# Keeping the last three items' rows apart, and scaling and storing the sums one item earlier

## What is computed

```
y = x + attention(...)                         # these rows start the sums, acc
h = rms_norm(y); gates = softmax(top-4 of 32 of (h @ router_w + router_b))
for expert e, for the rows that chose e:
    gu  = h_rows @ w_gu[e] + b_gu[e]           # 1024 -> 2048
    act = min(gu_a, 7) * sigmoid(1.702 * min(gu_a, 7)) * (clip(gu_b, -7, 7) + 1)
    acc[rows] += gate * (act @ w_down[e] + b_down[e])
out = acc * rsqrt(mean(acc ** 2) + 1e-5) * final_norm_g
```

## Time and profile before

| | |
|---|---|
| median of 3 runs | 2220.52 us (2220.04 to 2221.96) |
| the profiled execution, its own time | 2224.10 us |
| its span, first to last instruction | 2222.3 us |
| TensorE busy | 2179.7 us, 98% of the span |
| mean granted TensorE clock | 0.992 of full speed |
| VectorE, ScalarE, GpSimd busy | 1384.9, 568.5, 253.1 us |
| DMA | 489.55 MB, mean 220 GB/s |

### The profile page before, as it was taken

The page is one execution under the profiler, slowest core; times in us unless marked ns, Lnnn a source line. Parts: engine busy times, 40 slices in busy tenths (PEclk is TensorE's granted clock), DMA queues, the critical chain, the costliest instruction groups (busy, mean ns, idle before and its releaser), DMA issues.

```text
span 2222.3 us, 39903 instructions
## 1 busy us (share of the span) xinstructions
PE 2179.7 (98%) x14798; PEld 1896.8 (85%) x14799; DVE 1384.9 (62%) x2827; ACT 568.5 (26%) x1247; POOL 253.1 (11%) x229
## 2 busy tenths in 40 slices
PE   9999999999999999999999999989999999999996
PEld 7444554566579999999999999989999999999996
DVE  3352232677667778776877678745766566667566
ACT  2113121345312222222222222211212122222123
POOL 1000000022140010101010101000100000011003
PEclk9999999999999999999999999999999999999998
DMA  8000001211158999898999899956977788789687
GB/s 319 33 38 1 0 11 65 88 43 58 49 206 280 313 313 306 288 304 298 307 300 325 272 305 312 315 192 221 307 246 229 235 283 284 251 288 314 221 301 287
DMA packets 244660, 489.55 MB, mean 220 GB/s; under 512 B 24399, under 2 KB 24607, under 8 KB 244452
## 3 DMA queue, kind: packets, MB, share of 16 engines
q1 hardware_dynamic: 223684, 452.48, 58.9%
q0 software_dynamic: 20704, 36.29, 6.9%
q10 hardware_dynamic: 224, 0.16, 0.0%
HBM read 477.64 MB, written 49.63 MB: 237 GB/s over the span
## 4 chain that ended last, share of the span: by engine, by line
PE 94%; issue 2%; DMA 2%; DVE 1%; ACT 1%; POOL 0%; SPq 0%; POOLq 0%; DVEq 0%
PE PS L1042 68%; PE PS L690 14%; PE PS L898 5%; PE PS L698 1%; PE PS L871 1%; PE PS L838 1%; PE PS L860 1%; PE PS L917 0%; PE PS L705 0%; DVE unit L1599 0%; DMA acc_dram<-pairA,cur_y 0%; DMA pairB<-acc_dram 0%; DMA out_dram<-pairB 0%; DMA unit<-acc_dram,cur_y 0%; PE PS L783 0%
## 5 line engine op out<-in xcount | busy, mean ns | idle before, releaser
L1042 PE MATMUL PS<-pairA,unit 128*128 x12288 | 1543.5, 289 | 16.4 <-issue 15.3
L1042 PEld LDWEIGHTS PS<-pairA,unit 128*128 128x128 f32 x12288 | 1538.3, 191 | 21.7 <-issue 20.6
L1810 DVE STREAM_TRANSPOSE unit<-unit 32x512 f32<-32x512 f32 x496 | 315.3, 636 | 8.2 <-DMA unit<-h_dram,cur_x 1.4
L1829 DVE STREAM_TRANSPOSE pairA<-unit 32x512 f32<-32x512 f32 x496 | 315.3, 636 | 6.9
L1349 ACT ACTIVATE unit<-PS,cur_b 128x256 f32<-128x256 f32 x256 | 107.2, 470 | 398.2 <-PE PS L1042 353.0
L690 PE MATMUL PS<-pairA,unit 128*128 128x512 f32 (+1 forms) x464 | 202.9, 594 | 0.0
L1330 ACT ACTIVATE unit<-unit 128x512 f32<-128x512 f32 x128 | 80.5, 630 | 470.2 <-DVE unit L1868 470.1
L1336 ACT ACTIVATE unit<-PS,cur_b 128x256 f32<-128x256 f32 x256 | 107.2, 470 | 308.7 <-PE PS L1042 304.9
L583 POOL DMA_INDIRECT acc_dram<-pairA,cur_y x62 | 99.3, 1601 | 701.8 <-ACT pairA L1309 691.6
L690 PEld LDWEIGHTS PS<-pairA,unit 128*128 128x128 f32 (+1 forms) x464 | 85.6, 187 | 101.1 <-issue 100.3
L1883 DVE TENSOR_SCALAR unit<-unit 128x512 f32<-128x512 f32 x128 | 54.5, 426 | 158.6 <-ACT unit L1336 155.3
(11 more groups left out here) (259 smaller groups left out, 1194.2 us busy)
## 6 DMA issues: line engine op xcount, KB each, us to landing
unit<-in_expert_w_gu_dram SPq DMA_DIRECT2D x256, 1024.0 KB, 5.4
unit<-in_expert_w_down_dram SPq DMA_DIRECT2D x128, 1024.0 KB, 7.9
unit<-in_w_in_dram SPq DMA_DIRECT2D x6, 2048.0 KB, 14.7
pairB<-in_x_dram SPq DMA_DIRECT2D x16, 512.0 KB, 12.0
unit<-in_w_out_dram SPq DMA_DIRECT2D x2, 2048.0 KB, 8.9
h_dram<-pairA SPq DMA_DIRECT2D x8, 512.0 KB, 2.6
acc_dram<-pairB SPq DMA_DIRECT2D x8, 512.0 KB
pairB<-acc_dram SPq DMA_DIRECT2D x8, 512.0 KB, 8.0
```

The source lines that it names most:

```text
L1042: ins = pe.matmul(ps[:, ITEM * (j % 2):ITEM * (j % 2) + w], slot_w[s][:, k, P * j:P * j + P], xa_cols[:, ITEM * kd:ITEM * kd + KD * ITEM + ...
L1810: ins = dve.transpose(cols[:, :, :, 32 * q:32 * q + 32], rows[:, :, :, 32 * a:32 * a + 32])
L1829: ins = dve.transpose(rows[:, :, :, 32 * a:32 * a + 32], cols[:, :, :, 32 * q:32 * q + 32])
```

## The change

- Three items' rows are kept apart: item 29's too, in `old_rows`, with its indices copied to `old_y`. So the sums are read back one item earlier, with items up to 28 in them: SP loads tiles 0 to 2 among item 29's down slabs and 3 to 7 among item 30's first five slabs.
- ACT squares the tiles in item 30: three after `take_y`, two in its second pass, three behind its last read of the up half. DVE makes the mean and scales tiles 0 to 5 between item 30 and item 31, tile 6 in item 31's first pass and tile 7 in its second. In item 31 ACT squares `old_rows` (in place of six tiles), and DVE scales them after tile 7.
- SP stores the eight tiles among item 31's slab loads: tile 0 behind slab (0, 2), 1 and 2 behind (0, 3), 3, 4, 5 behind (1, 0), (1, 1), (1, 2), 6 behind (2, 0) and 7 behind (2, 2). Each store waits in SP's queue until its tile is scaled, and the next slab's load stands behind it.
- POOL gathers `old_rows` in item 30, after the adds have landed and ahead of its `y_sent`, makes one more power ahead of item 31's adds, and at the end writes three sets of rows in place of two, each after the one before has landed (`y_out`). A memset of `old_rows` is added ahead of POOL's loop.
- Item 30 is written out behind the loop on DVE, ACT and POOL, as item 31 was, and item 29 and 30 on SP. TensorE's program is unchanged.

```diff
@@ -200,6 +200,7 @@
         last_rows, prior_rows = kn(unit[5][:, 0:2048], 2), kn(unit[5][:, 2048:4096], 2)
+        old_rows = kn(unit[1][:, 1024:3072], 2)
@@ -430,7 +431,11 @@
-            def item_weights(i, e, sums=()):
+            def store_tile(t):
+                sp.wait_ge(out_ready, t + 1)
+                sp.dma_start(out_rows[t], acc[:, t, :]).then_inc(out_sent, 16)
+
+            def item_weights(i, e, sums=(), done=()):
@@ -439,33 +444,36 @@
                                 if t == 0:
-                                    sp.wait_ge(y_sent, last)
+                                    sp.wait_ge(y_sent, i + 2)
                                 sp.dma_start(acc[:, t, :], acc_dram[P * t:P * t + P, :]).then_inc(rows_in[t], 16)
+                        for t, place in done:
+                            if place == (p, s):
+                                store_tile(t)
...
                     load_slab(p, s, 0)
-            with sp.Fori(1, N_EXP - 2) as i:
+            with sp.Fori(1, N_EXP - 3) as i:
...
             item = sp.alloc_register("sp_item")
-            sp.reg_mov(item, N_EXP - 2)
+            sp.reg_mov(item, N_EXP - 3)
...
                 with sp.Fori(0, MAX_EXTRA):
-                    i = sp.snap(item, min_val=N_EXP - 2, max_val=ITEMS - 2)
-                    with sp.If(i + 2 < last):
+                    i = sp.snap(item, min_val=N_EXP - 3, max_val=ITEMS - 3)
+                    with sp.If(i + 3 < last):
...
                         sp.reg_add(item, item, 1)
-            prior = sp.snap(item, min_val=N_EXP - 2, max_val=ITEMS - 2)
-            e = sp.value_load(item_e[0:1, bass.ds(prior, 1)], min_val=0, max_val=N_EXP - 1)
-            item_weights(prior, e, ((0, (2, 1)), (1, (2, 2)), (2, (2, 3))))
-            e = sp.value_load(item_e[0:1, bass.ds(prior + 1, 1)], min_val=0, max_val=N_EXP - 1)
-            item_weights(prior + 1, e, ((3, (0, 0)), (4, (0, 1)), (5, (0, 2)), (6, (0, 3)), (7, (1, 0))))
-            for t in range(NT):
-                sp.wait_ge(out_ready, t + 1)
-                sp.dma_start(out_rows[t], acc[:, t, :]).then_inc(out_sent, 16)
+            old = sp.snap(item, min_val=N_EXP - 3, max_val=ITEMS - 3)
+            loads = (((0, (2, 1)), (1, (2, 2)), (2, (2, 3))),
+                     ((3, (0, 0)), (4, (0, 1)), (5, (0, 2)), (6, (0, 3)), (7, (1, 0))), ())
+            stores = ((), (), ((0, (0, 2)), (1, (0, 3)), (2, (0, 3)), (3, (1, 0)), (4, (1, 1)), (5, (1, 2)),
+                               (6, (2, 0)), (7, (2, 2))))
+            for n in range(3):
+                e = sp.value_load(item_e[0:1, bass.ds(old + n, 1)], min_val=0, max_val=N_EXP - 1)
+                item_weights(old + n, e, loads[n], stores[n])
@@ -603,30 +611,46 @@
             last = pool.value_load(n_items[0:1, 0:1], min_val=N_EXP, max_val=ITEMS)
+            pool.memset(old_rows, 0.0)
...
                         i = pool.snap(item, min_val=1, max_val=ITEMS)
-                        with pool.If(i + 1 < last):
+                        with pool.If(i + 2 < last):
...
                             pool.reg_add(item, item, 1)
-            final = pool.snap(item, min_val=N_EXP - 1, max_val=ITEMS - 1)
-            for t in range(NT):
-                pool.wait_ge(rows_in[t], 32)
-            add_to_sums(final)
-            pool.wait_ge(mean_sq, 3 * NT + 1)
-            pool.tensor_tensor(rstd[:, :], ssq[:, :], neg_half[:, :], ALU.pow).then_inc(rstd_ready, 1)
-            pool.wait_ge(y_out, 32 * final)
-            pool.sem_inc(pool_waited, 1)
-            for rows, index, arrived in ((prior_rows, cur_y, prior_in), (last_rows, cur_x, xg_in)):
+
+            def take_rows(rows, index, arrived):
+
+                pool.sem_inc(pool_waited, 1)
...
+
+            prior = pool.snap(item, min_val=N_EXP - 2, max_val=ITEMS - 2)
+            next_rows(prior)
+            for t in range(NT):
+                pool.wait_ge(rows_in[t], 32)
+            add_to_sums(prior)
+            step.do(pool.tensor_copy(old_y[:, :], cur_y[:, :]))
+            pool.wait_ge(y_out, 32 * prior)
+            take_rows(old_rows, old_y, apart_in)
+            pool.sem_inc(y_sent, 1)
+
+            pool.wait_ge(mean_sq, 3 * NT + 1)
+            pool.tensor_tensor(rstd[:, :], ssq[:, :], neg_half[:, :], ALU.pow).then_inc(rstd_ready, 1)
+            pool.wait_ge(apart_in, 32)
+            pool.wait_ge(mean_sq, 3 * NT + 2)
+            pool.tensor_tensor(small[:, 10:12], small[:, 8:10], neg_half[:, 0:2], ALU.pow).then_inc(rstd_ready, 1)
+            add_to_sums(prior + 1)
+            pool.wait_ge(y_out, 32 * prior + 32)
+            take_rows(prior_rows, cur_y, apart_in)
+            take_rows(last_rows, cur_x, xg_in)
@@ -637,21 +661,24 @@
-            pool.wait_ge(mean_sq, 3 * NT + 2)
+            pool.wait_ge(mean_sq, 3 * NT + 3)
...
             for b in range(2):
-                finish_rows(prior_rows, cur_y, b, NT + b + 1)
+                finish_rows(old_rows, old_y, b, NT + b + 1)
+            pool.wait_ge(y_out, 32 * last)
             for b in range(2):
-                pool.wait_ge(mean_sq, 3 * NT + 3 + b)
+                finish_rows(prior_rows, cur_y, b, NT + b + 3)
+            for b in range(2):
+                pool.wait_ge(mean_sq, 3 * NT + 4 + b)
...
                                    ALU.pow).then_inc(rstd_ready, 1)
-            pool.wait_ge(y_out, 32 * last)
+            pool.wait_ge(y_out, 32 * last + 32)
             for b in range(2):
-                finish_rows(last_rows, cur_x, b, NT + 3 + b)
-            pool.wait_ge(prior_in, 32)
+                finish_rows(last_rows, cur_x, b, NT + 5 + b)
+            pool.wait_ge(apart_in, 64)
             pool.wait_ge(xg_in, 32 * last + 64)
-            pool.wait_ge(y_out, 32 * last + 32)
+            pool.wait_ge(y_out, 32 * last + 64)
@@ -1318,17 +1345,21 @@
-            def gate_up(i, first=False, final=False):
+            def gate_up(i, first=False, prior=False, final=False):
...
                 if final:
-                    square_sums(range(6))
+                    act.wait_ge(apart_in, 32)
+                    for b in range(2):
+                        square_rows(old_rows[:, b, :], small[:, 8 + b:9 + b], NT + b)
...
                                        scale=ALPHA).then_inc(sig_ready, 1)
+                    if p == 1 and prior:
+                        square_sums(range(3, 5))
@@ -1339,8 +1370,8 @@
                         take_y(i)
-                    if p == 0 and final:
-                        square_sums(range(6, NT))
+                    if p == 0 and prior:
+                        square_sums(range(3))
@@ -1360,24 +1391,28 @@
                         i = act.snap(item, min_val=1, max_val=ITEMS)
-                        with act.If(i + 1 < last):
+                        with act.If(i + 2 < last):
...
                             act.reg_add(item, item, 1)
-            final = act.snap(item, min_val=N_EXP - 1, max_val=ITEMS - 1)
+            prior = act.snap(item, min_val=N_EXP - 2, max_val=ITEMS - 2)
             for s in range(SLOTS):
-                take_down(s, 3 * final)
-            gate_up(final, final=True)
-
-            act.wait_ge(prior_in, 32)
+                take_down(s, 3 * prior)
+            gate_up(prior, prior=True)
+            square_sums(range(5, NT))
+            for s in range(SLOTS):
+                take_down(s, 3 * prior + 3)
+            gate_up(prior + 1, final=True)
+
+            act.wait_ge(apart_in, 64)
             for b in range(2):
-                square_rows(prior_rows[:, b, :], small[:, b:b + 1], NT + b)
+                square_rows(prior_rows[:, b, :], small[:, b:b + 1], NT + 2 + b)
...
                 act.wait_ge(last_summed, 2 * b + 2)
-                square_rows(last_rows[:, b, :], small[:, 2 + b:3 + b], NT + 2 + b)
+                square_rows(last_rows[:, b, :], small[:, 2 + b:3 + b], NT + 4 + b)
@@ -1859,6 +1894,7 @@
                         turn_y(i, (2, 3))
+                        mean_of(small[:, 8:10], NT + 2)
@@ -1871,13 +1907,14 @@
                         turn_y(i, (2, 3))
-                    if p == 1 and final:
-                        mean_of(ssq[:, :], NT)
...
                     if p == 1 and final:
-                        norm_sums(range(3))
+                        norm_sums((7,))
+                        dve.wait_ge(rstd_ready, 3 * NT + 2)
+                        for b in range(2):
+                            norm_rows(old_rows[:, b, :], small[:, 10 + b:11 + b])
@@ -1888,6 +1925,8 @@
                         turn_rows(i + 1, (2 * p, 2 * p + 1))
+                    elif p == 0:
+                        norm_sums((6,))
@@ -1949,7 +1988,7 @@
                         i = dve.snap(item, min_val=1, max_val=ITEMS - 1)
-                        with dve.If(i + 1 < last):
+                        with dve.If(i + 2 < last):
@@ -1957,7 +1996,15 @@
                             dve.reg_add(item, item, 1)
-            final = dve.snap(item, min_val=N_EXP - 1, max_val=ITEMS - 1)
```

(25 more changed lines are left out.)

## The result

The changed kernel took 2224.89 us (median of 22 runs, 2219.99 to 2227.57), the kernel before on the same chip 2221.20 (22 runs). The ratio is **1.0014, 95% interval [1.0008, 1.0020]**: some 3.1 us slower (it is not the ratio of the two medians, which lie 3.7 us apart). Predicted were 2.9 us less, and 2225 was outside the range. The difference is within the 0.2% that was called no change, but on the other side, and with 22 runs it can be told from none.

The account below looks back on a forecast made before the run. TensorE was taken to bound the kernel, busy 98% of the span, leaving the ends to win, where stores and writes follow. Terms -3.8 + 0.9 + 0 = -2.9 took the median from 2220.52 to 2217.6 us, range 2215.8 to 2221.6.

Parts of the forecast that it names:

- Moved: eight stores among the slab loads: Item 31's slab loads: TensorE ends 0.5 us later, hidden beside GpSimd's delay; 0 us, bounds 0 and +1.6.
- TensorE starves: Rival at slabs (1, 3) to (2, 1): stores not absorbed, TensorE 8.5 us late, time 2225.2; chance 0.10.
- Removed: the stores behind the last slab: Kernel's end: with the stores sent early, the last rows' second write starts at 2212.4 for 2216.14; -3.8 us.
- Added: a third set of rows, and the delay of that row: GpSimd's final writes: three sets in turn, delayed 1.3 us, end 0.9 behind the last rows' path; +0.9 us.
- GpSimd never waiting for the stores: Sign that the forecast is right, at GpSimd's final writes: no wait for the stores of the sums; no size given.
- Everything else at nothing: Items 29 to 31: earlier scaling, squares, tile waits, written-out item 30 and memset fit in idle time; costed at nothing.
- All of it: Rival at the kernel's end: adds land as before, power at 1.03; -3.8, 2216.7; chance 0.12 for below 2216.1.

Follow-up runs that it names:

- no stores: Changed kernel without the eight stores of the sums and the waits on them; median 2217.50 us, ratio 0.9978 to the kernel before.
- after, again: Changed kernel, unedited, profiled a second time; its last write starts 74.77 us after the issue of item 31's first slab.
- last two at (2, 3): Changed kernel with only the stores of tiles 6 and 7 put behind the last slab; median 2223.92 us, ratio 1.0017 to before.
- plain adds: Changed kernel with item 31's two adds writing over the sums (bypass) in place of adding; median 2220.33 us, ratio 0.9995 to before.
- six stores earlier: Changed kernel with tiles 0 to 5 stored behind slabs (0, 1) to (1, 0), 6 and 7 behind (2, 3); 2218.89 us, ratio 0.9995 to before.

## Why the prediction was wrong, and where right

**The step that failed is "Moved: eight stores among the slab loads", costed at 0 us with +1.6 as its bound.** It measured +8.4 on TensorE's end. Of these 4.11 + 1.07 are waits, 6.28 - 3.57 = 2.7 is the slab at half clock, and 0.5 is spread over others. With -3.3 for the tail the end came 5.1 later. This was the first rival, "TensorE starves", which had 8.5 us and 2225.2 and the chance 0.10. The sizes agree, and that is in part luck: its 8.5 had no half clock in it, and its 2225.2 meets the median of 2224.89 only because some 2 us of item 31's 5.1 don't show in the whole kernel. The mechanism agrees only in part, as follows.

The step took the queue as one pipe with a mean rate, and its backlog as a sum of bytes. The trace has 16 semaphore events for each slab's load, one for each part of the transfer, and TensorE waits for the last. The core has 16 DMA engines; the events don't name one, and I take each part to be one engine's. For slab (1, 2), us from issue, in order of arrival:

```
no stores               4.5  4.5  4.7  4.7  4.8  4.8  4.8  4.9  4.9  4.9  4.9  4.9  4.9  4.9  5.0  5.0
after                   7.7  7.7  7.8  7.8  7.8  7.8  7.9  7.9  7.9  7.9  8.0  9.4 14.4 14.5 14.5 15.0
after, again            7.6  7.6  7.6  7.6  7.6  7.7  7.7  7.7  7.8  7.9  7.9  7.9 13.0 14.7 14.8 15.4
last two at (2, 3)      7.7  7.8  7.8  7.9  7.9  7.9  7.9  7.9  8.0  8.0  8.0  8.0  8.0  8.0  8.1 14.9
plain adds              7.4  8.2  8.6  8.8  8.9  8.9  9.0  9.0  9.1  9.1  9.2  9.2  9.2  9.4  9.8 10.0
six stores earlier      6.4  6.4  6.5  6.5  6.5  6.5  6.5  6.5  6.6  6.6  6.7  6.7  6.7  6.8  7.8 10.0
```

By the prediction's own count slab (1, 2) should land after 5.4 + 1.75 + 2 x 0.42 = 8.0 us. Eleven or twelve parts do, within 0.4. Four do not (in one kernel a single one), and these decide. They fall behind at slab (0, 3), where two stores follow one slab: its last parts land at 8.5 and 8.6 where the others need 5.8. They keep that distance, at 10.1 and 10.3 in the next two slabs against 7.4 and 7.7: the DMA engines were busy for 0.70 of 2160 to 2162, and from 2164 on for all of the time, so whoever was behind had no gap to catch up in. When the adds move (issued at 2171.21 and 2173.16) the distance grows to 6.5. The slab that came too late was therefore (1, 2), 4.3 us past its 10.7, and not (1, 3), for which the step had 0.5.

Which cause has which share: without the stores there is no lateness, with plain adds 3.2 of 8.4 stay, with the stores earlier 0.2 to 1.4. The two act together, and the shares don't simply add. That the adds stretch the gap of the engines already behind is read from two profiles of the changed kernel and one of its neighbour; the kernel with plain adds had no such group even before its adds were issued, so it does not prove that step. Why some engines fall behind, and why four, is open. So is 2 us of the balance: the changed kernel loses 5.1 in item 31 by the profiles and 3.1 by the runs, and the profiles of all changed kernels reach item 31 at 2140.0 to 2144.7, the two of before at 2144.8 and 2147.2. Two profiles of before can't tell a lead from scatter.

**Not in the sum: SyncE held up by its own issue.** Tile 6's store took 4.16 us to issue (0.4 to 1.6 for the others). TensorE left slot 1 at 2179.3, and slab (2, 1) was issued at 2181.64 only, 2.3 late; it landed at 2197.55, and the second wait, 1.07 us, was for it. What the late issue cost isn't shown: without that store at this place slab (2, 0) kept TensorE waiting for 1.02, and with plain adds, where the same store took 0.36 to issue, (2, 1) kept it waiting for 2.42.

**Not in the sum either: what a wait costs beyond itself.** A wait of 4.11 us brought 2.7 us of loss at half clock behind it.

**Removed: the stores behind the last slab** (-3.8): -3.3 (-3.9 against the second profile of before), right in kind and nearly in size. The last write was to start 3.7 us behind the mean of the last rows, and started 4.1 behind it (2218.03 - 2213.89). The 0.4 comes by way of the second power, 1.53 us beside VectorE's scaling where the earlier trace rows have 1.11 for two:

```profile
2213.81 1.27 DVE L1875 SCALAR_TENSOR_TENSOR unit<-unit,small 128x1024 f32<-128x1024 f32 x1
2215.53 1.28 DVE L1875 SCALAR_TENSOR_TENSOR unit<-unit,small 128x1024 f32<-128x1024 f32 x1 [0.45 <-POOL small L674]
```

The power started at 2213.97, 0.16 behind the first scaling, and ended at 2215.50, 0.42 behind its end, so the second scaling began 0.45 late. The first write, started at 2215.90 beside it, took 1.83 us and ended 0.92 after the scaling's end at 2216.81; the write of before took 1.28 and ended 0.90 after its scaling; others take 0.97. So both kinds wait for VectorE, as I read these times. The Trainium skill, "SBUF — State Buffer", "Who interferes with whom", says that a VectorE instruction with two inputs in SBUF and a GpSimd instruction that reads SBUF exclude each other. For the power the trace agrees: 1.53 us beside the scaling, and 0.58 for the same power free of it. Where the power lies beside a scaling was not in the prediction.

**Added: a third set of rows, and the delay of that row** (+0.9): the power ahead of the writes shrank as taken (0.72, predicted 1.03). A pair of writes took longer: 5.95 us from its start to the next pair's (2202.79 to 2208.74), where the sum has 1.34 + 3.1 + 0.9 = 5.3. The row could be seen alone only where TensorE was on time: +0.7 without stores, and some 1.9 with the stores early (the last write 9.1 behind TensorE), GpSimd's wait of 3.71 us for tiles 6 and 7 included. The second add took 9.4 us to land where it had taken 9.04, +0.4 in place of +1.0. In the changed kernel all of it hid behind TensorE's 8.4. "GpSimd never waiting for the stores" was wrong: it waited 5.53 us, because the stores, issued early, landed late.

**Everything else at nothing** held. The six tiles were scaled by 2157.69. `cur_b` was copied at 2158.53, 14.53 us after item 31's first slab was issued, the same as in the earlier trace rows, and VectorE had waited 0.77 us for ScalarE there, so the scaling held nothing up.

**All of it** (-3.8, 2216.7) is near what the kernel without stores shows, 2217.5, and -4.9 by its ratio of 0.9978. Only the number agrees: that kernel stores nothing, in item 31 it gains 2.6 and not 3.8, and GpSimd's row of writes sets its end.

## What to carry to other kernels

A wait for a transfer ends with its last part. A queue near the 394 GB/s seen here can't be counted in bytes alone: of a slab's 16 parts one to four fell 3 us behind, and they stayed behind through the next slabs, as no gap came in which to catch up. Put extra transfers where the queue drains between two loads, and ahead of the traffic that will slow it, rather than spread evenly up to it; here six of eight stores one or two slabs earlier, and the seventh a slab later, turned +0.14% into -0.12%. Price a wait of the bounding engine with the clock that it loses.

## What the runs showed of the hardware that was not expected

- Parts of one DMA drift apart under load and stay apart: 5.8 and 8.6 us after the issue in one slab, 7.9 and 15.0 three slabs on.
- While the adds that accumulate move, the other queue moves less, and so do both together. From 2176.5 to 2182 in the changed kernel (queue, packets, MB, share of 16 engines), 0.59 MB of adds and 1.02 MB of everything else in 5.5 us, 294 GB/s together where 403 to 410 were moved just before:

```profile
q0 software_dynamic: 272, 0.59, 54.9%
q1 hardware_dynamic: 446, 1.02, 49.5%
```

- TensorE's granted clock fell from 2.4 to 1.2 GHz in or behind waits of 4.11, 4.17 and 3.58 us (the last began 7.4 us after one of 1.41 had ended), and did not behind one of 3.55 us. In the second profile of the changed kernel:

```profile
2180.00:2182.00 2.00, 0.28 (x1) 0.50 1.05 409
2182.00:2184.00 2.00, 2.00 (x10) 0.50 1.04 414
```

- The issue of a store held its engine for 4.16 and 4.17 us in the two profiles of the changed kernel, with slabs (1, 2) to (2, 0) not yet landed. With plain adds the same store took 0.36 us.
